# A two-stream pooling and state-space layer: tables turned and powers built ahead of the token loop, three turned-token buffers, the first projected blocks by token group, all first states copied by ScalarE

## The reference

```
h    = rmsnorm(x) * (1 + sc1) + sh1             # scale/shift from silu(cond) @ w_ada
proj = h @ w_in                                  # 1024 x 1024
pool = per-group map of windowed mean minus token  (first 512 channels)
bu   = b_bar u ;  h_t = a_bar h_{t-1} + bu       # 32 groups, 64 complex states, both directions
y    = Re(C_f h_f) + Re(C_b h_b) + D u ; gelu, sigmoid GLU  (last 512 channels)
x    = x + g1 * (concat(pool, y) @ w_out)
x    = x + g2 * (relu(rmsnorm(x) ... @ w_mlp1)**2 @ w_mlp2) ; final rmsnorm
```

## Time and profile before

| | |
|---|---|
| time, median of 3 runs | 1355.71 us (1355.52 to 1356.09) |
| profiled execution | 1355.27 us, span 1353.5 us |
| TensorE busy | 1227.0 us, 91% of the span |
| VectorE busy | 859.0 us, 63% |
| ScalarE busy | 327.8 us, 24% |
| GpSimd busy | 456.8 us, 34% |
| moved by transfers | 101.63 MB, mean 75 GB/s |

### The profile page before, as it was taken

How to read it: one execution, slowest core, us unless ns; L and a number is a source line. 1 busy time by engine, 2 the same in 40 slices (tenths; PEclk the granted TensorE clock), 3 DMA queues, 4 the chain that set the end, 5 groups by cost and what they waited for, 6 DMA issues and landing times.

```text
span 1353.5 us, 18586 instructions
## 1 busy us (share of the span) xinstructions
PE 1227.0 (91%) x6479; PEld 1060.9 (78%) x6479; DVE 859.0 (63%) x1353; ACT 327.8 (24%) x594; POOL 456.8 (34%) x367
## 2 busy tenths in 40 slices
PE   3869898677995797999999999999999999999994
PEld 0169896454764786998998998998998898899893
DVE  1679799877991748646546546645645645655648
ACT  2372324314221447400110110110110110110013
POOL 1100001100100043165356347347337437536536
PEclk9969899788998899999999999999999999999998
DMA  8814143643454351212101102101101101101003
GB/s 197 287 32 94 61 82 114 226 68 103 84 156 121 76 170 55 71 32 62 39 23 62 46 16 62 53 25 46 62 21 41 62 31 31 62 31 31 31 0 139
DMA packets 82633, 101.63 MB, mean 75 GB/s; under 512 B 28322, under 2 KB 65350, under 8 KB 82340
## 3 DMA queue, kind: packets, MB, share of 16 engines
q1 hardware_dynamic: 60864, 81.38, 20.5%
q0 software_dynamic: 4448, 16.29, 4.3%
q10 hardware_dynamic: 17284, 3.47, 1.3%
HBM read 89.53 MB, written 9.49 MB: 73 GB/s over the span
## 4 chain that ended last, share of the span: by engine, by line
PE 76%; DVE 11%; issue 3%; ACT 3%; DMA 3%; POOL 2%; ACTq 1%; POOLq 0%; DVEq 0%
PE bank L1262 22%; PE bank L1263 22%; PE bank L1264 22%; POOL acc L477 2%; DMA raw<-in_w_ada 2%; PE bank L1275 1%; PE bank L1440 1%; PE bank L1439 1%; DVE x_lo L888 1%; DVE w_lo L892 1%; ACTq L491 1%; PE bank L1391 1%; ACT x_hi L520 1%; DVE fold_p L991 1%; PE bank L1454 1%
## 5 line engine op out<-in xcount | busy, mean ns | idle before, releaser
L477 POOL TENSOR_TENSOR acc<-acc,gated 128x512 f32<-128x512 f32 x288 | 401.3, 1393 | 391.1 <-DVE gated L1226 352.1
L1262 PE MATMUL bank<-x_hi,w_hi 128*128 128x384 f32 x992 | 334.9, 338 | 26.3 <-issue 18.3
L1263 PE MATMUL bank<-x_lo,w_hi 128*128 128x384 f32 x992 | 333.4, 336 | 0.0
L1264 PE MATMUL bank<-x_hi,w_lo 128*128 128x384 f32 x992 | 333.2, 336 | 0.0
L1226 DVE TENSOR_TENSOR gated<-bank,gate_b 128x512 f32<-128x512 f32 x288 | 193.9, 687 | 116.6 <-PE bank L1264 100.5
L1262 PE MATMUL bank<-w_hi,f_hi 128*128 128x512 f32 x576 | 224.3, 389 | 0.6 <-DVE gated L1226 0.6
L1264 PE MATMUL bank<-w_hi,f_lo 128*128 128x512 f32 x576 | 224.4, 390 | 0.0
L1263 PE MATMUL bank<-w_lo,f_hi 128*128 128x512 f32 x576 | 224.4, 390 | 0.0
L1262 PEld LDWEIGHTS bank<-x_hi,w_hi 128*128 128x128 f32 x992 | 187.8, 189 | 27.5 <-issue 18.7
L775 ACT ACTIVATE relu<-bank 128x384 f32<-128x384 f32 x96 | 47.2, 493 | 650.5 <-PE bank L1264 648.9
L1216 DVE TENSOR_TENSOR f_tmp<-relu 128x384 f32<-128x384 f32 x96 | 65.7, 685 | 213.8 <-ACT relu L775 213.5
(11 more groups left out here) (283 smaller groups left out, 1246.8 us busy)
## 6 DMA issues: line engine op xcount, KB each, us to landing
raw<-in_w_mlp SPq DMA_DIRECT2D x64, 512.0 KB
raw<-in_w_ada SPq DMA_DIRECT2D x48, 512.0 KB
x_tile<-in_x_sample POOLq DMA_DIRECT2D x8, 512.0 KB, 8.5
raw<-in_w_in SPq DMA_DIRECT2D x8, 512.0 KB
raw<-in_w_out SPq DMA_DIRECT2D x8, 512.0 KB
x_again<-in_x_sample POOLq DMA_DIRECT2D x8, 512.0 KB, 4.5
out<-acc SPq DMA_DIRECT2D x8, 512.0 KB, 2.6
u_rows<-proj ACTq DMA_DIRECT2D x4, 576.0 KB, 2.8
```

What stands on the lines that cost most here:

```text
L477: GP.tensor_tensor(a, a, BT[i % 4][:], ALU.add).then_inc(s.acc, 1)
L1262: mm(out, sh_, mh, start=first, stop=False)
L1263: mm(out, sh_, ml, start=False, stop=False)
L1264: return mm(out, sl, mh, start=False, stop=last)
```

## The change

- The turning of the parameter tables and first states stands on TensorE behind the fifth unit of w_ada, where it stood behind the eighth and its bias.
- On VectorE the power chain and one of the eight `to_state` calls, (1, 1, 0), stand ahead of the normalizing; the other seven stay behind the token loop, in a new order with the weight splits.
- There are three turned-token buffers, and the odd tiles use banks 6 and 7, not 2 and 3. TensorE therefore waits ahead of tile 1 for the columns to be read out.
- The first six projected blocks go by token group (both column blocks of group 0, then of group 1, then of group 2), and the first two of them are issued in pieces behind tiles 4 to 8 of the token loop.
- ScalarE copies out all 16 first states; VectorE none.
- Some small tiles are placed together, which changes no instruction's work.

```diff
-WB_AT = {(1, 0): (0, 1), (1, 1): (2, 3), (1, 2): (4, 5), (2, 0): (6, 7),
-         (3, 0): (8, 9), (3, 1): (10, 11), (3, 2): (12, 13), (4, 0): (14, 15)}
+WB_AT = {3: (0, 1), 4: (2, 3), 5: (4, 5), 6: (6, 7), 9: (8, 9), 10: (10, 11), 11: (12, 13), 12: (14, 15)}
+IN_SEQ = [(i, g) for g in range(NG) for i in range(2)] + [(i, g) for i in range(2, 8) for g in range(NG)]
+IN_END = {i: a for a, (i, g) in enumerate(IN_SEQ)}
+BESIDE = {4: (0, 0, 3), 5: (0, 3, 6), 6: (0, 6, 8), 7: (1, 0, 3), 8: (1, 3, 8)}
...
-    HT0 = [at(f"h_tile{i}", [P, KB, P], R_S + i * 4 * KBYTE) for i in range(2)]
+    HT0 = [at(f"h_tile{i}", [P, KB, P], o) for i, o in enumerate((R_S, R_P, R_P + 10 * KBYTE))]
...
-    def turn_banks(t, odd):
-        return (BANK[4], BANK[5]) if t % 2 == 0 else (BANK[odd], BANK[odd + 1])
+    def turn_banks(t):
+        return (BANK[4], BANK[5]) if t % 2 == 0 else (BANK[6], BANK[7])
...
-            if base + t >= 2:
-                act.wait_ge(s.h_lo, base + t - 1)
+            n = len(ht)
+            if base + t >= n:
+                act.wait_ge(s.h_lo, base + t - n + 1)
...
-                    act.wait_ge(s.in_mm, 3 * (w - 1))
+                    act.wait_ge(s.in_mm, IN_END[w - 2] + 1)
...
         act.wait_ge(s.ada0, 2)
+        act.wait_ge(s.tabs, 4)
         affine(0, HT0, 0, 0)
...
-        for i in range(N_IN):
-            for g in range(NG):
-                project(NG * i + g)
-                for k in WB_AT.get((i, g), ()):
-                    turned_wb(k)
-            if i + 2 < N_IN:
+        for a in range(NG * N_IN):
+            i, g = IN_SEQ[a]
+            project(a)
+            for k in WB_AT.get(a, ()):
+                turned_wb(k)
+            if g == NG - 1 and i + 2 < N_IN:
                 split_hi(i + 2, FIRST_IN + i + 2)
-            if i == 2:
-                act.wait_ge(s.wbt, 8)
-                for p_ in range(0, 16, 2):
+            if a == 8:
+                for p_ in range(16):
+                    if p_ == 9:
+                        act.wait_ge(s.wbt, 7)
                     states_out(p_)
...
-            tt(out, out, tmp, ALU.add).then_inc(s.wbt, 1)
-            dve.wait_ge(s.wbt, 4 * b + 2 * d + h + 1)
+            tt(out, out, tmp, ALU.add).then_inc(s.wbt if ready else s.wbt_first, 1)
+            dve.wait_ge(s.wbt if ready else s.wbt_first, max(ready, 1))
...
+        V.tensor_copy(H0S[:], BANK[6][:, 4 * Q:5 * Q]).then_inc(s.h0_ready, 1)
...
+        power_chain()
+        to_state(1, 1, 0, 0)
         for t in range(TT):
             normed(t, XS[t][:], XS[t][:], 0)
...
         dve.wait_ge(s.h_lo, TT)
-        to_state(0, 0, 0)
-        to_state(0, 0, 1)
+        to_state(0, 0, 0, 1)
+        to_state(0, 0, 1, 2)
+        to_state(0, 1, 0, 3)
         split_lo(2, FIRST_IN + 2)
-        to_state(0, 1, 0)
-        to_state(0, 1, 1)
-        power_chain()
+        to_state(0, 1, 1, 4)
+        to_state(1, 0, 0, 5)
         split_lo(3, FIRST_IN + 3)
-        for d in range(2):
-            for h in range(2):
-                to_state(1, d, h)
+        to_state(1, 0, 1, 6)
+        to_state(1, 1, 1, 7)
         split_lo(4, FIRST_IN + 4)
-        for p_ in range(1, 16, 2):
-            states_out(p_)
-        dve.wait_ge(s.st_act, 8)
+        dve.wait_ge(s.st_act, 16)
...
                 ada_unit(part * KB + k, (2 * part, 2 * part + 1), k)
+                if part == 0 and k == 4:
+                    pe.wait_ge(s.tabs, 3)
+                    for i in range(4):
+                        last = PE.transpose(BANK[6][:, i * Q:(i + 1) * Q], TAB[:, i, :], ID[0:Q, 0:Q])
+                    last.then_inc(s.pe_small, 1)
...
-        for t in range(TT):
-            turn_tile(t, XS[t], 0)
-
-        def project(a):
-            i, g = a // NG, a % NG
-            if g == 0:
-                pe.wait_ge(s.w_split, i + 1)
+        def project(a, k0, k1):
+            i, g = IN_SEQ[a]
+            if k0 == 0:
+                if g == 0:
+                    pe.wait_ge(s.w_split, i + 1)
+                if i == 0:
+                    pe.wait_ge(s.h_lo, 3 * (g + 1))
...
+        for t in range(TT):
+            if t == 1:
+                pe.wait_ge(s.h0_ready, 1)
+                pe.wait_ge(s.ada0, 2)
+            turn_tile(t, XS[t], 0)
+            if t in BESIDE:
+                project(*BESIDE[t])
...
-        for i in range(N_IN):
-            for g in range(NG):
-                project(NG * i + g)
-                for k in WB_AT.get((i, g), ()):
-                    turn_wb(k)
-            if i == 2:
+        for a in range(2, NG * N_IN):
+            project(a, 0, KB)
+            for k in WB_AT.get(a, ()):
+                turn_wb(k)
+            if a == 8:
                 for p_ in range(16):
                     states(p_)
```

More of the change, by code:

```diff
@@ L116, in build @@
     COL = at("vector_cols", [P, 36], R_C + 9984)
-    EPSB = at("eps", [P, 1], R_C + 10144)
-    CSG = at("c_sign", [P, 1], R_C + 10176)
-    ONE = at("ones", [1, 2], R_C + 10208)
-    STAT = [at(f"stat{i}", [P, TT], R_C + 10240 + 64 * i) for i in range(3)]
-    H0S = at("first_states", [P, Q], R_C + 10336)
+    CONST = at("constants", [P, 4], R_C + 10144)
+    EPSB, CSG, ONE = CONST[:, 0:1], CONST[:, 1:2], CONST[0:1, 2:4]
+    STATS = at("stats", [P, 3, TT], R_C + 10176)
+    STAT = [STATS[:, i, :] for i in range(3)]
+    H0S = at("first_states", [P, Q], R_C + 10304)
     PROJ = [at(f"proj{i}", [P, L, CH], R_U + 9216 + i * 4608) for i in range(2)]
@@ L841, in _, with to_state @@
         V.tensor_copy(TAB[:, :, N:P], TAB[:, :, 0:N]).then_inc(s.tabs, 1)
-        def to_state(b, d, h):
+        def to_state(b, d, h, ready):
             gs = slice(b * GB + 8 * h, b * GB + 8 * h + 8)
@@ L936, in _, with power_chain @@
         dve.wait_ge(s.tabs, 4)
+        def power_chain():
+            then(V.tensor_copy(AQ[0:N, :], PI[0:N, L, :]))
+            then(ts(AQ[N:P, :], PI[N:P, L, :], -1.0, None, ALU.mult))
+            sr, si = (v.rearrange("p (d b g) -> p d b g", d=2, b=2) for v in (PR[:, L, :], AQ[:]))
+            for i in range(6):
+                dr, di = AR_[i][:], AI_[i][:]
+                if i == 0:
+                    dr, di = (v.rearrange("p (b d g) -> p d b g", d=2, b=2) for v in (dr, di))
+                then(tt(dr, sr, sr, ALU.mult))
+                then(tt(di, si, si, ALU.mult))
+                then(tt(dr, dr, di, ALU.subtract))
+                then(tt(di, sr, si, ALU.mult))
+                then(ts(di, di, 2.0, None, ALU.mult))
+                sr, si = AR_[i][:], AI_[i][:]
+        power_chain()
+        to_state(1, 1, 0, 0)
         for t in range(TT):
@@ L1283, in _ @@
                 ada_unit(part * KB + k, (2 * part, 2 * part + 1), k)
+                if part == 0 and k == 4:
[3 more added lines that the diff above has]
+                    last.then_inc(s.pe_small, 1)
+                    pe.wait_ge(s.str_ready, 1)
+                    PE.transpose(BANK[6][:, 4 * Q:5 * Q], STR[:].rearrange("q r n -> q (r n)"), ID[0:Q, 0:Q]).then_inc(s.pe_small, 1)
             for hf in range(2):
@@ L1287, in _ @@
             last.then_inc(s.ada_mm, 1)
-            if part == 0:
-                pe.wait_ge(s.tabs, 3)
-                for i in range(4):
-                    last = PE.transpose(BANK[6][:, i * Q:(i + 1) * Q], TAB[:, i, :], ID[0:Q, 0:Q])
-                last.then_inc(s.pe_small, 1)
-                pe.wait_ge(s.str_ready, 1)
-                PE.transpose(BANK[6][:, 4 * Q:5 * Q], STR[:].rearrange("q r n -> q (r n)"), ID[0:Q, 0:Q]).then_inc(s.pe_small, 1)
         for k in range(4):
@@ L1307, in turn_tile @@
             for k in range(KB):
-                last = PE.transpose(turn_banks(t, 6 if base else 2)[k // 4][:, (k % 4) * P:(k % 4 + 1) * P], src[:, k * P:(k + 1) * P], ID[:])
+                last = PE.transpose(turn_banks(t)[k // 4][:, (k % 4) * P:(k % 4 + 1) * P], src[:, k * P:(k + 1) * P], ID[:])
             last.then_inc(s.tr, 1)
-        for t in range(TT):
-            turn_tile(t, XS[t], 0)
-        def project(a):
-            i, g = a // NG, a % NG
-            if g == 0:
-                pe.wait_ge(s.w_split, i + 1)
+        def project(a, k0, k1):
+            i, g = IN_SEQ[a]
+            if k0 == 0:
+                if g == 0:
+                    pe.wait_ge(s.w_split, i + 1)
+                if i == 0:
+                    pe.wait_ge(s.h_lo, 3 * (g + 1))
+                if a >= 4:
+                    pe.wait_ge(s.in_ev, a - 3)
+                else:
+                    pe.wait_ge(s.row_ready, a + 1)
@@ L1318, in project @@
             wh = WH[i % 2][:].rearrange("p (k f) -> p k f", k=KB)
             wl = WL[i % 2][:].rearrange("p (k f) -> p k f", k=KB)
-            if i == 0:
-                pe.wait_ge(s.h_lo, 3 * (g + 1))
-            if a >= 4:
-                pe.wait_ge(s.in_ev, a - 3)
-            else:
-                pe.wait_ge(s.row_ready, a + 1)
-            for k in range(KB):
+            for k in range(k0, k1):
```

(13 more changed lines are left out.)

52 lines of the change are left out of this document (13 added, 39 removed).

## The result

| | before | after |
|---|---|---|
| time, median of 4 runs each | 1355.62 us (1355.33 to 1356.09) | 1348.28 us (1345.56 to 1352.04) |
| profiled execution | 1355.27 us, span 1353.5 us | 1352.04 us, span 1350.0 us |
| VectorE busy | 859.0 us | 853.8 us |
| ScalarE busy | 327.8 us | 331.1 us |

The ratio is 0.9945, with a 95% interval of 0.9929 to 0.996: 7.3 us faster. The forecast was 1341.6, that is 14 us faster; the measured time lies in the range of 1338 to 1350.5, but outside the forecast's own 1338 to 1346. The profiled execution of the kernel after is the slowest of its four: its span is 3.5 us shorter, where the medians differ by 7.3, so its rows show about half of the usual gain. A second execution of the same kernel was therefore profiled too (the first experiment).

What follows compares the result with a forecast made beforehand. Bound: engine hops ahead of the first scan, in table turning, token loop, VectorE's late tables and a scan wait. Scan 13.3 us earlier, both engines 14.1 after its split: 1355.27 less 14.1, plus 0.4, gives 1341.6 us; range 1338 to 1346, with half-clock loop 1350.5.

Steps and rivals of the forecast that it cites:

- a half clock through the loop: Rival in the token loop: alternating pieces and tiles keep TensorE's clock half; second block 8.9 us late, 1350.5 us; chance 0.12.
- The chunks' way through memory starts at block six's eviction and moves with it: Between second block and first states: chunks come earlier along with TensorE's blocks, the ninth at 128.0; no separate size given.
- behind the last tables nothing waits: Ahead of the first states: VectorE is through near 130, so ScalarE's 3.98 us wait for the last table is gone.
- here no pause comes ahead: First states: no TensorE pause precedes them, unlike before; 16 take 7.8 us and the scan starts at 138.0, 13.3 us earlier.
- The token loop: With three buffers a tile costs some 2.6 us, not 3.80; after 4.6 us of half clock, second block ends at 95.3.
- neither half-clock rival: Half clock through the token loop (1350.5 us, chance 0.12), or lasting into blocks three to nine (up to 1375.7, chance 0.04).
- The 7.2 us credited to the pieces: Token loop: three buffers and pieces between tiles end the second block at 95.3; ScalarE picked it up at 102.56 before.
- Columns: Ahead of the token loop: early turning, powers and one to_state leave the columns' effect at 0, bound +0.6 us.
- First states on ScalarE: Ahead of the first scan: ScalarE, free at 130.1, copies all 16, 0.49 us a pair, 7.8 us in all.
- The split inside the scan: First scan: VectorE waits 1.6 us for a high weight half in place of 2.42, TensorE being 14.1 us earlier.
- a constant shift of 14: Sign of being right: after the scan's first split, everything stays 14 us earlier; a shrinking shift after 230 us means wrong.
- The gain is handed back: Rival after the scan: transfers or GpSimd don't move along; 1355.7 us, half handed back 1348.6; chance 0.06.

Runs made afterwards that it cites:

- powers_alone: The kernel before with only the table turning behind the fifth unit and the power chain ahead of the norms (second turned-token buffer moved): 1354.23 us, ratio 0.9986.
- load6_behind: The changed kernel with the seventh w_in load behind the chunk loads on SyncE's queue, not ahead: 1343.15 us, ratio 0.9914.
- same_again: The changed kernel once more, unaltered, with a second profile (span 1348.2 us): 1349.12 us, ratio 0.9946 to the kernel before.
- no_pieces: The changed kernel without pieces of blocks between the tiles; blocks one and two run whole after all nine tiles: 1348.83 us, ratio 0.9956.
- turn_sooner: The changed kernel with the seventh w_in load behind the chunks, pieces one tile later, and table turning behind w_ada's fourth unit: 1341.28 us, ratio 0.9894.
- powers_late_load6: The changed kernel with the seventh w_in load behind the chunks, and power chain and first to-state table back behind the token loop: 1351.33 us, ratio 0.9961.
- pieces_later: The changed kernel with the pieces one tile later, behind tiles 5 to 8, the whole second block behind tile 8: 1345.39 us, ratio 0.993.
- load6_pieces_later: The changed kernel with both the seventh w_in load behind the chunks and the pieces one tile later: 1342.75 us, ratio 0.9908.

## Why the prediction was right, and where it was short

- **Direction: right; the bound: half right.** With VectorE's late work away, ScalarE goes from the ninth block into the first states, VectorE waits for it (11.86 us at 146.15), and the scan starts 5.15 us sooner. But VectorE's late work was not the bound by itself: powers_alone took 8.05 us of it away and moved the scan by 1.3.
- **The range was met partly by luck.** The measured gain is half of the forecast. The range reaches up to 1350.5 for a half clock through the loop, and that did not come. The collision that took the gain is in no rival.
- **The step that fell short: "The chunks' way through memory starts at block six's eviction and moves with it", and with it "behind the last tables nothing waits".** It looked only at when the way starts, not at what shares it. The sum has weight transfers go out when a buffer comes free, "so they move too"; one of them moved the other way, by 5.7 us. The write met this 512 KB load, took 6.2 us and not 2.8, and TensorE waited 3.95 us. Shown by load6_behind: one load behind the chunks gives 6.0 us of median back, 1343.15 against a forecast of 1341.6.
- **"here no pause comes ahead"** failed with it. The pause came, the clock was 0.50 for some 5.5 us after it, and the first states cost 2.1 us more. In load6_behind, with a pause of 0.8, the clock was 1.00.
- **The token loop: right in mechanism and size.** The clock rose within the loop, as forecast, and neither half-clock rival came. Counted from the columns, the first piece started 0.5 us sooner than forecast (83.32, where 81.2 was put, with columns 2.7 late), the half clock lasted 5.7 us (up to 89) and not 4.6, and the second block ended 0.2 late. The low halves of tiles 5 to 7 came 2.9, 2.4 and 2.4 us behind the one before, where 2.6 was put. The row at 98.54 holds the last two low halves, and the last was through at 101.03, 2.5 later than the 98.5 forecast, much as the columns. (The forecast's own terms for it, 86 + 4 x 2.6 + 1.2, give 97.6.)
- **The 7.2 us credited to the pieces was too simple.** The bookkeeping is right (the second block's successor is picked up earlier) but nearly the same comes with no pieces at all: no_pieces picks that block up at 96.62. The sum gave one number to "three buffers, pieces of blocks" and never asked for each alone. No run takes away the third buffer alone, so that it brings this gain is argued from the low halves, 2.4 us apart and not 3.80, and not shown.
- **Columns: bound too narrow.** The forecast took 0 with a bound of +0.6; the first profile has +2.7 (70.10 against 67.44), the second +1.25. The sum from the first power copy on was right: from it to the norms pass 27.5 us (34.06 to 61.57), where 27.7 were forecast. What was off is its start. TensorE began with w_ada at 21.97 and not 20.88, and the first five units took 11.60 and not 10.25 us, so the fifth was through at 33.57 and not 31.13. The first 1.1 us are one parameter transfer, which ScalarE took 10.63 us to issue and 9.53 in the kernel before; it is 9.61 in same_again. VectorE then came to the column scaling at 69.33 without a wait, 1.6 us behind TensorE's last rows (67.11 + 0.58). The forecast had seen this case as 0.6 at most.
- **First states on ScalarE: as forecast.** One engine is enough at full clock.
- **The split inside the scan: 2.60 us, where 1.6 was forecast.** The shift of TensorE and that of the scan are the same, so the wait stays; about 1 us of size.
- **"a constant shift of 14" and "The gain is handed back": a small part is.** The forecast named a shrinking shift after 230 us as a sign of being wrong, and it is there. Starts in us, with the second scan taken at its first fold of states_b and the MLP at its first relu:

| | first scan | second scan | MLP | end of span |
|---|---|---|---|---|
| before | 151.30 | 335.78 | 554.89 | 1353.5 |
| after | 146.15 | 331.19 | 551.43 | 1350.0 |
| turn_sooner | 135.80 | 319.99 | 542.08 | 1340.6 |

From the second scan to the MLP pass 219.1 us before, 219.4 in powers_alone, 219.5 in powers_late_load6, and 220.2 to 222.1 in the other nine traces; from the MLP to the end it is 798.5 to 798.6 in all three rows. In the kernel after, the largest single loss is 0.9 us, where TensorE starts again behind an idle time of 18 us, at 443.54 before and 438.61 after: from this start to its next one (474.87 and 470.79) pass 31.3 and 32.2 us. The clock four microseconds behind the start, first before, then after (columns as in the earlier trace rows):

```profile
447.50:449.50 2.00, 2.00 (x14) 2.00 (x13) 0.66 (x1) 2.00 (x2) 0.00 (x0) 1.00 0.92 348
```

```profile
442.60:444.60 2.00, 2.00 (x9) 2.00 (x9) 0.93 (x1) 2.00 (x3) 0.00 (x0) 0.61 1.01 387
```

The clock came back later there. Whether that follows from the change or from the execution is open.

The rule of the Trainium skill weighed in the prediction ("TensorE: Matmul & The Clock Gate", Part 4, PE-mode transpose: transposes don't engage the full clock) is not borne out by these runs either. Alternating tiles and pieces brought the clock from 0.50 to 1.00 by 90, and in pieces_later tile 6 was turned in 1.03 us, behind one piece, where at half clock a tile takes 1.9. Here matmuls stand between the transposes; the row that has transposes alone is that of the kernel before, 66.6 to 73 us.

## What to carry to other kernels

When a change moves work, list the transfers that each moved step releases, on every queue, and look at which of them now fall together; a write whose reader is on the path shouldn't meet a large load that nobody needs yet. A new order of blocks moves both: the work that comes sooner and the split that frees a buffer later. Price each part of a change alone and with its partners: early powers were worth 2 us alone and, with one early table, some 6 to 8 with the rest in place, the pieces nothing that the medians show. And look at what a wait ahead of TensorE does to its clock: here the waits of 3.2 us and more at the first states were paid twice, for themselves and for the half clock behind them.

## What the runs showed of the hardware

- A write of 576 KB from ScalarE's queue (144 packets in the profile), issued 1.2 us behind a 512 KB load from SyncE's queue (1,040 packets), took 6.2 us to land (5.7 and 6.1 in two other traces); apart from such a load it took 2.8 (before) and 3.1 (load6_behind). The profile lists the two queues apart, and each engine was done issuing in under 0.4 us.
- After a pause of 3.95 us at full clock, TensorE ran at 0.50 up to 140, over 5 us of uninterrupted work, and first states came every 0.96 us and not every 0.49. After one of 3.19 us (same_again) it ran at 0.50 up to 135, under 3 us. After pauses of 2.66 (pieces_later), 1.42 (load6_pieces_later) and 0.8 us (load6_behind) the clock stayed at 1.00; but in powers_alone, after one of 2.53 us ahead of its fifth step of first states (139.83), it was 0.50 up to 146. So the length of the pause alone doesn't tell these cases apart.
- ScalarE took 9.53 us to issue one parameter transfer in one execution and 10.63 in another (before and after, the same instruction), and all that stood behind it came 1.1 us later.
- Two profiles of one kernel differ by 3.8 us at the first scan (146.15 and 142.38): 1.4 at the columns, the rest at the chunks. A single profile places a stage no better than that here.
